# The second block's output projection as three fp32r products, with its copies and low parts spread over the attentions

## The reference

```python
z = jnp.einsum('bsd,de->bse', _rmsnorm_2(x, norm_g[l]), w_in[l])
q_a, k_a, v_a, g_a, q_b, ..., v_d, g_d = jnp.split(z, offs, axis=-1)
o_a = _dense_blocked(...)      # rms-normed heads, axial rotation
o_b = _window_sink(...)        # rotation, window mask, sink
o_c = _neighbourhood(...)      # bias from a table
o_d = _diff_blocked(...)       # difference of two softmaxes, then rms norm
mix = concatenate([o_a * silu(g_a), o_b * silu(g_b), o_c * silu(g_c), o_d * silu(g_d)])
x = x + jnp.einsum('bsm,md->bsd', mix, w_out[l])
```

## Time and profile before

| | |
|---|---|
| median of 3 runs | 1157.89 us (1157.75 to 1158.03) |
| profiled execution | 1157.58 us, its span 1155.5 us |
| TensorE (PE) busy | 1126.9 us, 98% |
| TensorE weight loads (PEld), beside PE | 1013.9 us, 88% |
| VectorE busy | 767.5 us, 66% |
| ScalarE busy | 524.1 us, 45% |
| GpSimd busy | 65.7 us, 6% |

### The profile page before, as it was taken

The page is one execution under the profiler, slowest core; times in us unless marked ns, Lnnn a source line. Parts: engine busy times, 40 slices in busy tenths (PEclk is TensorE's granted clock), DMA queues, the critical chain, the costliest instruction groups (busy, mean ns, idle before and its releaser), DMA issues. The chain is left out here.

```text
span 1155.5 us, 21951 instructions
## 1 busy us (share of the span) xinstructions
PE 1126.9 (98%) x9400; PEld 1013.9 (88%) x9400; DVE 767.5 (66%) x1104; ACT 524.1 (45%) x734; POOL 65.7 (6%) x51
## 2 busy tenths in 40 slices
PE   5999999999999999999999999999999999999997
PEld 4789989899999998798998999999997768877785
DVE  5587765867565665787665965556667685677744
ACT  5355443534333344465334443333355565446642
POOL 1002000100000000011001000000001100030000
PEclk9999999999999999999999999999999999999999
DMA  9543335445354355443335355534436234353320
GB/s 358 222 163 110 116 109 188 176 164 224 159 218 187 144 199 187 146 146 111 111 111 220 109 219 219 216 140 189 181 141 229 109 111 182 115 218 134 116 79 37
DMA packets 27610, 188.16 MB, mean 163 GB/s; under 512 B 3472, under 2 KB 4368, under 8 KB 5776
## 3 DMA queue, kind: packets, MB, share of 16 engines
q1 hardware_dynamic: 25952, 175.89, 40.7%
q10 hardware_dynamic: 1440, 8.55, 1.9%
q0 software_dynamic: 144, 2.66, 0.6%
HBM read 181.84 MB, written 5.24 MB: 162 GB/s over the span
## 5 line engine op out<-in xcount | busy, mean ns | idle before, releaser
L669 PE MATMUL bank<-in_low,h_high 128*128 128x512 f32 x352 | 138.3, 393 | 0.0
L669 PE MATMUL bank<-in_high,h_high 128*128 128x512 f32 x288 | 117.5, 408 | 12.5 <-DVE in_low L1977 11.8
L1089 PE MATMUL bank<-h_high,gate_split 128*128 128x256 f32 x704 | 128.8, 280 | 0.2
L1089 PE MATMUL bank<-h_high,up_split 128*128 128x256 f32 x704 | 128.6, 280 | 0.0
L1105 PE MATMUL bank<-act_split,down_split 128*128 128x256 f32 x960 | 118.4, 283 | 0.0
L1105 PEld LDWEIGHTS bank<-act_split,down_split 128*128 128x128 f32 x960 | 116.6, 192 | 0.0
L694 PE MATMUL bank<-h_high,in_high 128*128 128x256 f32 x384 | 115.8, 302 | 0.5 <-DVE in_low L1851 0.5
L1378 ACT ACTIVATE in_high<-ring 128x2048 fp32r<-128x2048 f32 x47 | 89.6, 1910 | 54.9 <-PE bank L669 53.6
L669 PE MATMUL bank<-in_high,x_low 128*128 128x512 f32 x288 | 113.1, 393 | 0.0
L1089 PEld LDWEIGHTS bank<-h_high,gate_split 128*128 128x128 f32 x704 | 109.9, 189 | 0.9 <-DVE h_low L1793 0.6
L1089 PEld LDWEIGHTS bank<-h_high,up_split 128*128 128x128 f32 x704 | 109.8, 189 | 0.0
(11 more groups left out here) (348 smaller groups left out, 2385.2 us busy)
## 6 DMA issues: line engine op xcount, KB each, us to landing
ring<-w_in_dram SPq DMA_DIRECT2D x71, 1024.0 KB, 4.9
ring<-w_gate_up_dram SPq DMA_DIRECT2D x44, 1024.0 KB, 8.3
ring<-w_down_dram SPq DMA_DIRECT2D x22, 1024.0 KB, 4.8
ring<-w_out_dram SPq DMA_DIRECT2D x16, 1024.0 KB, 6.5
ring<-p_all_dram SPq DMA_DIRECT2D x6, 1024.0 KB, 4.8
x_kept<-scratch ACTq DMA_DIRECT2D x4, 1024.0 KB, 3.9
x<-x_kept ACTq DMA_DIRECT2D x4, 1024.0 KB, 8.4
table<-tables_dram POOLq DMA_DIRECT2D x1, 2594.0 KB, 11.9
```

The costliest lines, as they stand in the source:

```text
L669: last = mm(bank[(n - n % 2 + t) % 4][:], a, b, start=c == 0 and i == 0, stop=c == KT - 1 and i == 2)
L1089: last = mm(bank[2 * half + part][:, f * S:(f + 1) * S], a, b, start=k == 0 and i == 0, stop=k == KT - 1 and i == 2)
```

## The change

It does these things, in each layer of the second block. Where a diff has "...", lines are left out.

- The four output tiles get high parts (`out_high(q)` on ScalarE into `o2_high`) and low parts (`out_low(q, k)` on VectorE, in halves, in place in the ring: `o2_low`), the four mixed tiles too (`mixed_high(n)`, `mixed_low(n)`; the fourth from the bank itself). `piece` runs three fp32r matmuls where it ran one fp32 one, and waits for the low parts.
- Memory: the high parts of the mixed tiles 0 to 2 lie where `yT` and the lora weights lay, those of the output tiles in the scratch memory where the bias was (q = 0, 1; q = 3 again the first) and in `in_third`'s place (q = 2). Input tile 5 gets a fourth place, `in_fourth`, for its high part, for which ScalarE waits for no piece; VectorE makes its low part ahead of the wait for the roots of attention A's head norms (`b_rs`).
- The next layer's tiles 0 and 1 are split at the end of D and behind the next norm, no longer in D's rounds.
- ScalarE's lists: in B the gate's copy goes between the exponentials of heads 0 and 1 and the tile copy behind the two weight copies; the tanh before B goes ahead of the pair's scaling.

```diff
@@ memory, signals @@
+        in_fourth = nc.alloc_sbuf_tensor_at("in_fourth", [P, KT, 256], F32R, offset=yT_at + 4 * 512)
+        def high_of(l, n):
+            return in_fourth if n == 5 else high2[l][n % 3]
...
+        o2_low = [nc.alloc_sbuf_tensor_at(f"out2_low{q}", [P, 2, D], F32R, offset=ring_at + 8192 * SLOT2[G2 + q]) for q in range(4)]
@@ TensorE, piece @@
+                    pe.wait_ge(*o2_lo.after(l, 2 * q + (k + 1 if q < 3 else 2)))
+                    w = o2_high[q], o2_low[q]
+                    m_ = mix_high[q], mix_low[q]
...
+                        for m0 in range(0, KT, 2):
+                            for m in (m0, m0 + 1):
+                                for k in range(2):
+                                    for a in range(2):
+                                        part(m, k, a, 0)
+                            if m0 == 0:
+                                pe.wait_ge(*mx_lo.after(l, 4))
+                            for m in (m0, m0 + 1):
+                                for k in range(2):
+                                    last = part(m, k, 0, 1, m == m0 + 1 and k == 1)
+                            last.then_inc(wo2_end.sem, 1)
                         return
+                    pe.wait_ge(*mx_lo.after(l, q + 1))
                     for m in blocks:
-                        last = mm(bank[m // 2][:, m % 2 * S:(m % 2 + 1) * S], w[:, k, m * P:(m + 1) * P], mixT[q][:, k, :],
-                                  start=False, stop=False)
+                        for a, b in ((0, 0), (0, 1), (1, 0)):
+                            last = part(m, k, a, b)
@@ ScalarE @@
                 pair_out(l, 0)
-                next_high(l, 2)
+                in_split2(l, 5)
...
+                def out_high(q):
+                    s = SLOT2[G2 + q]
+                    act.wait_ge(*ring_in2[s].after(l, SLOT2[:G2 + q].count(s) + 1))
+                    f(o2_high[q][:], ring[:, s, :].rearrange("p (k n) -> p k n", k=2), ACT.Copy).then_inc(o2_hi.sem, 1)
+
+                def mixed_high(n):
+                    act.wait_ge(*b_mT.after(l, n + 1))
+                    f(mix_high[n][:], mixT[n], ACT.Copy).then_inc(mx_hi.sem, 1)
...
-                pair_out(l, 6)
                 act.wait_ge(*b_out.after(l, 6))
                 gate_sigmoid(l, 1280)
+                pair_out(l, 6)
 
                 exps, copy = attention(l, att, 4, 4, 1, lambda n: a_s[:, n % 2, :], sink=True)
                 exps(0)
+                gate_copy(1)
                 exps(1)
-                gate_copy(1)
-                next_high(l, 7)
                 copy(0)
                 copy(1)
+                next_high(l, 7)
+                mixed_high(0)
                 exps(2)
...
                 gate_sigmoid(l, 2304)
+                act.wait_ge(*bias_ok.after(l, 2))
+                out_high(0)
...
                 gate_copy(2)
+                mixed_high(1)
...
                 turned(l, 6, 256, 32 ** -0.5)
+                out_high(1)
...
                 fetch_x(l, x_saved2, x_back2)
+                mixed_high(2)
...
                 copy(0)
-                if l + 1 < DEPTH:
-                    in_split2(l + 1, 0)
+                out_high(2)
...
                 gate_sigmoid(l, 3072)
-                if l + 1 < DEPTH:
-                    in_split2(l + 1, 1)
+                act.wait_ge(*wo2.after(l, 1))
+                out_high(3)
...
                 f(b_t2, bank[7][:], ACT.Square).then_inc(b_lame.sem, 1)
-                y_copy(l, 3, b_mtp, mixT[3], bank[7], b_mT, 0.5)
+                if l + 1 < DEPTH:
+                    in_split2(l + 1, 0)
+                y_copy(l, 3, b_mtp, mix_high[3][:], bank[7], mx_hi, 0.5)
+                if l + 1 < DEPTH:
+                    act.wait_ge(*wo2.after(l, 3))
+                    in_split2(l + 1, 1)
@@ VectorE @@
-                in_split2(l, 2)
+                for n in range(1 if l else 2, 3):
+                    in_split2(l, n)
...
+                def mixed_low(n):
+
+                    dve.wait_ge(*mx_hi.after(l, n + 1))
+                    tt(mix_low[n][:], mixT[n], mix_high[n][:].bitcast(F32), ALU.subtract).then_inc(mx_lo.sem, 1)
+
+                def out_low(q, k):
+
+                    dve.wait_ge(*o2_hi.after(l, q + 1))
+                    tt(o2_low[q][:, k], ring[:, SLOT2[G2 + q], k * D:(k + 1) * D], o2_high[q][:, k].bitcast(F32), ALU.subtract)\
+                        .then_inc(o2_lo.sem, 1)
...
                 ts(st[:, 330:394], v2("subln"), v2("one_less"), None, ALU.mult)
+                in_split2(l, 5)
                 dve.wait_ge(*b_rs.after(l, 1))
...
-                for n in range(5, 7):
-                    in_split2(l, n)
+                in_split2(l, 6)
...
-                          splits={1: lambda l: in_split2(l, 9), 3: lambda l: in_split2(l, 10)})
+                          splits={1: lambda l: (in_split2(l, 9), mixed_low(0)), 3: lambda l: in_split2(l, 10)})
...
-                          splits={1: lambda l: in_split2(l, 12)})
+                          splits={1: lambda l: (in_split2(l, 12), mixed_low(1))})
...
                 rope(q_rot, q_t1, q_t2, qk6(2560), 6, "half", 16).then_inc(b_rot.sem, 1)
+                out_lows(0)
                 gated_turned(2)
+                out_lows(1)
...
-                          splits={3: lambda l: half_split2(l + 1, 0, 0), 5: lambda l: half_split2(l + 1, 1, 0)} if ahead else {},
-                          mixing={5: lambda l: half_split2(l + 1, 0, 1), 7: lambda l: half_split2(l + 1, 1, 1)} if ahead else {})
+                attention(l, att, 12, 8, 2, None, splits={1: lambda l: mixed_low(2), 5: lambda l: out_low(2, 1), 7: lambda l: out_low(3, 1)},
+                          mixing={5: lambda l: out_low(2, 0), 7: lambda l: out_low(3, 0)})
...
                 gated()
+                next_half(0, 0)
+                dve.wait_ge(*mx_hi.after(l, 4))
+                stt(mix_low[3][:], bank[7][:].rearrange("p (k s) -> p k s", k=2), 0.5, mix_high[3][:].bitcast(F32), ALU.mult, ALU.subtract)\
+                    .then_inc(mx_lo.sem, 1)
+                next_half(0, 1)
```

More of the change, by code:

```diff
@@ L197, in build @@
         lora = sb("lora", [P, 2, W4])
+        sb("after_lora", [P, 512])
         w_f = sb("w_f", [P, KT, NH])
@@ L442, in build @@
         b_mtp = goes_on(rt_q, 4)
-        b_mT = sig("b_mT", 4)
+        b_mT = sig("b_mT", 3)
+        o2_hi = goes_on(rt_T, 4)
+        o2_lo = goes_on(rt_s, 8)
+        mx_hi = goes_on(rt_txc, 4)
+        mx_lo = goes_on(rt_rqc, 4)
         rpb_in = sig("rpb_in", 1, 16)
@@ L523, in build @@
         mixT.append(yT[:, 0])
+        mix_high = [nc.alloc_sbuf_tensor_at(f"mix_high{q}", [P, 2, S], F32R, offset=yT_at + 4 * 512 * (q + 1)) for q in range(3)]
+        mix_high.append(ctx.enter_context(nc.sbuf_tensor("mix_high3", [P, 2, S], F32R)))
+        mix_low = [nc.alloc_sbuf_tensor_at(f"mix_low{q}", [P, 2, S], F32R, offset=arena_at + 4 * (D_IN2 * NT + 512 * q)) for q in range(3)]
+        mix_low.append(nc.alloc_sbuf_tensor_at("mix_low3", [P, 2, S], F32R, offset=yT_at))
+        o2_high = [nc.alloc_sbuf_tensor_at(f"out2_high{q}", [P, 2, D], F32R, offset=scratch_at + 4 * (4608 + 2048 * q)) for q in range(2)]
+        o2_high += [nc.alloc_sbuf_tensor_at("out2_high2", [P, 2, D], F32R, offset=scratch_at + 4 * 2560), o2_high[0]]
+        o2_low = [nc.alloc_sbuf_tensor_at(f"out2_low{q}", [P, 2, D], F32R, offset=ring_at + 8192 * SLOT2[G2 + q]) for q in range(4)]
         m_tmp = scratch[:, 4096:5120].rearrange("p (b c) -> p b c", b=2)
@@ L646, in split_operands @@
             def split_operands(n, l=None):
-                return (in_high[n % 2] if l is None else high2[l][n % 3]), in_low[n % 4]
+                return (in_high[n % 2] if l is None else high_of(l, n)), in_low[n % 4]
             def token_major(w, out, t):
@@ L1219, in piece, with part @@
                     s = SLOT2[G2 + q]
-                    if k == 0:
-                        pe.wait_ge(*ring_in2[s].after(l, SLOT2[:G2 + q].count(s) + 1))
                     if n == 2 * G2:
                         pe.wait_ge(*b_out.after(l, G2))
-                    w = ring[:, s, :].rearrange("p (k n) -> p k n", k=2)
-                    if n == 2 * G2:
                         for b in range(4):
                             mm(bank[b][:], zeros[:], h_high[:, 0:2, :].rearrange("p k s -> p (k s)"), start=True, stop=False)
+                    pe.wait_ge(*o2_lo.after(l, 2 * q + (k + 1 if q < 3 else 2)))
+                    w = o2_high[q], o2_low[q]
+                    m_ = mix_high[q], mix_low[q]
+                    def part(m, k, a, b, stop=False):
+                        return mm(bank[m // 2][:, m % 2 * S:(m % 2 + 1) * S], w[a][:, k, m * P:(m + 1) * P], m_[b][:, k, :],
+                                  start=False, stop=stop)
                     if q == 3:
@@ L1332, in _ @@
                 piece(l, 31, range(7, KT))
-                pe.wait_ge(*b_mT.after(l, 4))
+                pe.wait_ge(*mx_hi.after(l, 4))
                 piece(l, 32)
```

(5 more changed lines are left out.)

16 lines of the change are left out of this document (6 added, 10 removed).

## The result

The changed kernel takes 1168.78 us (median of 6 runs, 1166.73 to 1170.38) against 1157.69 (1157.42 to 1158.03, 6 runs): ratio 1.0095, 95% interval 1.0082 to 1.0108. Forecast was 1161.4 with a range to 1164.8: slower was right, the size wasn't, and the time lies outside the range. Two things stand out at once: the loss is three times the forecast one (+11.1 against +3.7), and the runs spread over 3.7 us where those of the kernel before lie within 0.6. The profiled execution took 1168.72, its span 1166.9 against 1155.5.

A forecast was written before the change was run, and what follows sets the result against it. TensorE, busy 98% of the span, was taken as the bound. Attention A +4.1, B +5.6, C +0.2, D and last pieces -6.4 gave +3.5 us: 1161.1 profiled, 1161.4 us as median, range 1157.0 to 1164.8.

The forecast's parts named there:

- The clock: Behind attention B's new 4.2 us gaps: no fall counted in the sum, though the skill's rule says both would be paid.
- the rotation in A: Attention A, layer 0: starts after tile 5's low part, takes 5.1 us as before and ends at 894.15, not 890.55.
- The products: Output projection: three fp32r products at 0.118 us each replace one fp32 matmul; 10.4 us less TensorE work.
- Attention D and the last pieces: Attention D gives 1.9 and 1.5 us, the last pieces 3.0 together: -6.4 us.
- the two waits walked out ahead: Attention D, from round three's half low part holding the next maxima: TensorE waits of 0.6 and 0.15 us.
- Attention C: Mixed tile 1's low part meets a VectorE idle time of 0.56 us: +0.1 us per layer, +0.2 in all.
- Attention B: Third head's maxima wait for mixed tile 0's low part and its ScalarE copy: 2.8 us per layer, +5.6 us.
- Rival 1: Attention B: mixed tile 0's copy reaches VectorE before it asks, so the kernel is faster, 1154.8 us; chance 0.12.
- rival 2: Attention B: the clock falls in the gaps, +1.7 us for one, +3.4 for both, 1163.1 to 1164.8; chance 0.22.
- Tile 5's low part (attention A): Moved ahead, it waits for ScalarE's copy and delays rotation and turning: 2.1 and 2.0 us, +4.1 in all.
- The sum: Whole kernel: 4.1 + 5.6 + 0.2 - 6.4 = +3.5 us on the profiled 1157.58.

The follow-up runs named there:

- the version with both back: Changed kernel with tile 5's low part back behind attention A's rotation and mixed tile 0's low part moved behind attention B: 1151.36 us, ratio 0.9947.
- The wait on GpSimd: Changed kernel with one more wait, holding GpSimd's bias addition back until attention A's rotation is done: 1166.19 us, ratio 1.0071.
- the version with the mixed low part moved: Changed kernel with mixed tile 0's low part moved on VectorE from behind head 1 of attention B to behind the gating after it: 1158.55 us, ratio 1.0006.
- with the clock and GpSimd out of play: Changed kernel with products of zeros filling TensorE's gaps in attentions A and B, and GpSimd's bias addition behind the rotation: 1161.26 us, ratio 1.0029.
- the first spread version: Kernel with both low parts back, attention D's half low parts spread from the first round on, copies of output tiles 2 and 3 a round earlier: 1159.03 us.
- the version with B's gap filled: Changed kernel with eight products of zeros on TensorE ahead of weighing 2 in attention B: 1166.98 us, ratio 1.0077.

## Why the prediction was wrong

Two steps failed. The clock was put at nothing in the sum, and its three falls cost 5.1 us; and the rotation in A was given its old durations at a new time, where GpSimd's addition cost it 2.0 us. The waits themselves, and what the products save, were read nearly right.

**The products**: right. 0.119 us each, as the earlier trace rows had it.

**Attention D and the last pieces**: right in sign and place, a little high. D gave 1.5 and 1.6 where 1.9 and 1.5 were forecast, the last pieces 1.2 and 1.3 where 1.5 was: -5.6 in all against -6.4. Of the two waits walked out ahead (0.6 and 0.15) both came in layer 0, behind a half low part that holds the maxima, at 0.27 and 0.18; in layer 1 only the first. The last values came 25.3 and 24.9 us after scores(0,1), forecast 25.0. (The 26.9 before is 26.84 in the rows, so 0.1 of the 1.9 is rounding.) For the last piece the forecast took its whole duration, 7.17, as what the fp32 matmuls cost; from its start to layer 1's second matmul it is 7.24 before and 6.01 after.

**Attention C**: right, 0.0 against 0.1 per layer.

**Attention B**: the idle time was right: 2.5 against 2.8 per layer, VectorE idle 2.7 us ahead of the mixed tile's low part, ended by ScalarE's copy. Rival 1 fell with it. What failed is what I said of the clock. "The gap is just as long as the time in which the clock was still full there" was used against rival 2 (0.22), and the gap came out shorter (3.7), yet the clock fell both times, at 1.6 and 1.5 us each. With zeros in the gap, the rest unchanged, the clock stayed full: that is shown. (The other row used for the clock, TensorE's start, rests on the spacing of its matmuls alone: the same view grants 1.00 from 11.77 to 15.28.) The Trainium skill (TensorE: Matmul & The Clock Gate, section Why this matters for your kernels) warns of idle gaps between matmul bursts, behind which the clock is back at half. These traces agree: it fell behind every gap of 2.81 to 5.17 us and behind 2.55 and 2.56, though not behind 2.78 in one execution. By that warning rival 2 was the likeliest case, at 1163.1 to 1164.8; I let one row from the end of the trace, with no work behind it, outweigh it.

**Tile 5's low part (attention A)**: this is where the forecast went most wrong, twice.
- The clock was weighed for B alone. The working says "TensorE idle 3 us before the turning" and doesn't put a fall beside it; it fell in layer 0 (0.6 us in the turning, 1.4 behind it), and in layer 1 of several variants. In layer 1 of the changed kernel's trace it didn't, and A cost the forecast 2.0.
- "The rotation ... now ends at 894.15" took the durations of the earlier trace rows for a rotation at a later time. There it met GpSimd's bias addition, whose start is set by a load and not by VectorE. The kernel before had this collision as well, on an instruction whose end nobody awaits. VectorE and GpSimd of the kernel before, and GpSimd of the version with both back:

```profile
894.96 2.87 DVE L2378 SCALAR_TENSOR_TENSOR scratch<-scratch,arena 128x512 f32<-128x512 f32 x1
...
893.15 6.94 POOL L2526 TENSOR_TENSOR scratch<-scratch,table 128x1024 f32<-128x1024 f32 x2 [7.75 <-DMA scratch<-rpb_dram]
```

```profile
893.37 6.81 POOL L2599 TENSOR_TENSOR scratch<-scratch,table 128x1024 f32<-128x1024 f32 x2 [7.88 <-DMA scratch<-rpb_dram]
```

The 2.87 us stands where the same line's instruction takes 0.69 in D (986.89 in the version with both back). It could have been seen. The move brought VectorE's rotation under the addition: 2.0 us more idle time in layer 0 of the profiled execution. The wait on GpSimd took 1.9 of them away: shown. It is a race of some tenths of a us, which VectorE won in the version with the mixed low part moved. The Trainium skill (SBUF — State Buffer, section Who interferes with whom) says that a VectorE instruction with two inputs in SBUF contends with a GpSimd instruction that reads SBUF, and the second to issue is blocked until the first is done. The three kinds that were hit here (0.96 to 2.95, 2.28 to 4.45, 0.69 to 2.87) are of that form, and each lost about the same 2.0 to 2.2 us, which agrees with a block better than with a slower rate. So does the end of the low part that took 4.45: it comes at 901.51, 2.15 us after GpSimd's two additions end (893.97 + 5.39 = 899.36), about its usual 2.28.

**The sum.** Forecast +3.5. The three falls of the clock add 5.1 by the ledger (4.5, and 0.6 in the turning), the collision 2.0, D and the last pieces 0.8, B takes 0.6 off, and 0.8 stood there before the block began: 3.5 + 5.1 + 2.0 + 0.8 - 0.6 + 0.8 = 11.6, less 0.2 of C: the 11.4 of the span. This is the account of one execution; others differ in which gaps brought a fall, in the race with GpSimd, and in the 0.8. The spread of the changed kernel isn't open: with the clock and GpSimd out of play it is 0.8 us in place of 3.7.

## What to carry to other kernels

An idle time of TensorE can have two prices, its length and a stretch at half clock behind it. Here the second came behind nearly every gap of 2.55 us or more, none of 1.6 or less, and was 1.0 to 2.8 us. So an edit that opens several waits has to be priced wait by wait against that length; a moved instruction has to be laid beside what GpSimd does at its new time. A low part belongs behind the copy that it needs and not ahead of work that TensorE waits for: with the two that stood wrong put back, the same products gave -0.5% in place of +1%.

## What the runs showed of the hardware

- The clock falls behind idle times much shorter than the 4.2 us that the end of the first trace suggested: 2.55 us was enough in one run, 2.78 not in another. A fall behind B's gap cost 1.5 and 1.6 us, some 6 to 8 matmuls at 0.42 in place of 0.23 between starts; one in A cost 2.0, the two in D of the first spread version 1.0 and 2.0, and one in A of the version with B's gap filled 2.8. Near that length it differs from run to run, and the kernel's spread is about 4 us where the kernel before has 0.6 to 1.5.
- Products of zeros in the waiting time held the clock: 2.1 us of them in a gap of 3.7, and the 1.6 us that were left caused no fall.
- Three fp32r products (0.36 us) are cheaper than one fp32 matmul of the same shape (0.43, two records), and TensorE's busy time counts a slow clock as work: it fell by 2.4 us in the changed kernel and by 8.2 with both low parts back, for the same products.
